# Residual stream held token by token: activations stationary in the out and down projections, LayerNorm per token, normalised tiles turned back

## The reference

```
x = first_block(x)                   # x += mixers(rms_norm(x)) @ w_out;  x += swiglu(rms_norm(x))
for i in range(4):                   # mixers: mLSTM, sliding window, HGRN2, differential attention
    for sub, f in enumerate((mixer[i], swiglu[i])):
        shift, scale, gate = split(silu(c) @ ada_w[i, sub] + ada_b[i, sub])     # 3 vectors of 1024
        h = x * (1 + scale) + shift
        x = layer_norm(ALPHA * x + (1 + gate) * f(h), ln_g[i, sub], ln_b[i, sub])
```

## Time and profile before

| | |
|---|---|
| runs | 3871.58, 3900.40, 3900.23 us, median 3900.23 |
| profiled execution: span | 3867.7 us |
| profiled execution: its own time | not given apart; the run nearest above its span is 3871.58, 3.9 us above it |
| PE busy | 3586.9 us, 93% |
| DVE, ACT, POOL busy | 1707.8 us (44%), 1205.6 us (31%), 1375.9 us (36%) |
| weight transfers | 501 of 512 KB, one of 501 slots each |

### The profile page before, as it was taken

The page is one execution under the profiler, slowest core; times in us unless marked ns, Lnnn a source line. Parts: engine busy times, 40 slices in busy tenths (PEclk is TensorE's granted clock), DMA queues, the critical chain, the costliest instruction groups (busy, mean ns, idle before and its releaser), DMA issues.

```text
span 3867.7 us, 44206 instructions
## 1 busy us (share of the span) xinstructions
PE 3586.9 (93%) x15724; PEld 2727.3 (71%) x15724; DVE 1707.8 (44%) x2681; ACT 1205.6 (31%) x1885; POOL 1375.9 (36%) x671
## 2 busy tenths in 40 slices
PE   7987999999879999899899999778999998989998
PEld 6754578886647888655688868665788875658886
DVE  2244345502155551554555232696654156553211
ACT  3235333222223222323333233332332231533322
POOL 3420034443304444300344434583344532024442
PEclk9868799999889999965899989989999988999998
DMA  4300045532204553200255423201455321012331
GB/s 136 98 22 1 20 144 186 193 113 77 76 0 138 184 186 128 85 17 1 82 195 189 143 79 102 64 1 53 145 184 179 113 79 60 1 44 87 98 98 66
DMA packets 101525, 374.07 MB, mean 97 GB/s; under 512 B 11280, under 2 KB 11408, under 8 KB 101136
## 3 DMA queue, kind: packets, MB, share of 16 engines
q1 hardware_dynamic: 101232, 371.76, 29.0%
q0 software_dynamic: 160, 0.52, 0.0%
HBM read 370.15 MB, written 2.10 MB: 96 GB/s over the span
## 4 chain that ended last, share of the span: by engine, by line
PE 79%; DVE 6%; ACT 2%; POOL 1%; issue 1%; DMA 0%; DVEq 0%; ACTq 0%; POOLq 0%
PE bank L602 18%; PE bank L604 18%; PE bank L603 18%; PE bank L787 4%; PE bank L807 3%; PE bank L690 2%; PE bank L691 2%; PE bank L692 2%; PE bank L795 2%; PE bank L646 1%; PE bank L648 1%; PE bank L647 1%; PE bank L992 1%; POOL hg_t L547 1%; DVE hg_d L1823 1%
## 5 line engine op out<-in xcount | busy, mean ns | idle before, releaser
L519 POOL TENSOR_TENSOR w_lo<-raw,w_hi 128x1024 fp32r<-128x1024 f32 x501 | 1230.8, 2461 | 2421.6 <-ACT w_hi L1086 2421.6
L1086 ACT ACTIVATE w_hi<-raw 128x1024 fp32r<-128x1024 f32 x501 | 527.8, 1058 | 1475.4 <-PE bank L604 1249.0
L602 PE MATMUL bank<-h_hi,w_hi 128*128 128x512 f32 x2392 | 934.6, 391 | 0.0
L604 PE MATMUL bank<-h_hi,w_lo 128*128 128x512 f32 x2392 | 931.8, 390 | 0.0
L603 PE MATMUL bank<-h_lo,w_hi 128*128 128x512 f32 x2392 | 931.5, 389 | 0.0
L602 PEld LDWEIGHTS bank<-h_hi,w_hi 128*128 128x128 f32 x2392 | 449.7, 188 | 94.3 <-issue 1.7
L604 PEld LDWEIGHTS bank<-h_hi,w_lo 128*128 128x128 f32 x2392 | 449.5, 188 | 94.2
L603 PEld LDWEIGHTS bank<-h_lo,w_hi 128*128 128x128 f32 x2392 | 449.7, 188 | 92.5
L1887 DVE SCALAR_TENSOR_TENSOR ada_acc<-ada_raw,cond,ada_acc 128x1024 f32<-128x1024 f32 x168 | 266.1, 1584 | 236.8 <-DMA ada_raw<-ada 235.6
L602 PE MATMUL bank<-hid_hi,w_hi 128*128 128x512 f32 x880 | 343.0, 390 | 0.4 <-DVE hid_lo L1903 0.4
L604 PE MATMUL bank<-hid_hi,w_lo 128*128 128x512 f32 x880 | 342.5, 389 | 0.0
...
## 6 DMA issues: line engine op xcount, KB each, us to landing
raw<-weights SPq DMA_DIRECT2D x501, 512.0 KB, 3.6
ada_raw<-ada SPq DMA_DIRECT2D x192, 512.0 KB, 4.4
layer_const<-layer_const SPq DMA_DIRECT2D x5, 512.0 KB, 4.4
...
```

The source lines that it names most:

```text
L519: nc.gpsimd.tensor_tensor(w_lo[k % RING][:, :, :], raw[k % RING][:, :, :], w_hi[k % RING][:, :, :].bitcast(F32), ALU.subtract).then_inc(sm ...
L602: mm(out, w_hi[r][:, at, :], hi, start=first and at == 0, stop=False)
L604: op = mm(out, w_lo[r][:, at, :], hi, start=False, stop=last and at == len(pairs) - 1)
L1086: fn(w_hi[t % RING][:, :, :], raw[t % RING][:, :, :], ACT.Copy).then_inc(sm.hi_done, 1)
```

## The change

x is held token-major, `[128, 4, 1024]`: token tile t has 128 tokens on the partitions and the 1024 features along the row. In the out and down projections the activations are now the stationary operand (128 features x 128 tokens) and the weights move (128 features x 512 output features). The output is made in two halves e = 0, 1 of 512 features. Within a half the four token tiles accumulate side by side in four banks, input chunk by input chunk (`token_chunk`: 12 products a chunk); in the last half the last four chunks go token by token (`last_half`), so that banks finish one after another. The weights are laid out by halves (`half_slots`); a down projection takes 22 slots instead of 24. The number of products is unchanged, 192 in an out projection and 528 in a down projection.

For each half and token tile DVE multiplies the bank by the gate row (L1587 of the changed kernel), adds ALPHA x (L1590) and takes BN_STATS of the 512 features (L1591). At e = 1 it aggregates the two (BN_AGGR, L1594), ACT takes a 128 x 1 root, DVE inverts it and writes the normalised token tile `xn` (128 x 1024, L1492). PE turns `xn` back to feature-major by 32 transposes of 128 x 128 (matrix products with the identity): 16 before the next projection (L743), 16 between its early products (L754). DVE applies scale and shift on reading the transposed banks (L1518). The gate is needed as a row: DVE writes eight diagonal tiles (L1541), PE spreads them by two float32 products with ones (L805, L806), DVE copies two banks (L1545). LayerNorm's own gain and bias reach x only later, two DVE operations of 128 x 1024 for each token tile, in the first eight `up` tiles of the feed-forward part or the first eight tiles of the next layer's input projection; for this `ln_rows` are loaded as broadcast rows, two transfers of 512 KB for each LayerNorm. After the last down projection gain and bias are applied token by token, each token tile stored by a transfer of its own. x is loaded by four transfers, and the first norm takes its squares on ACT token by token.

Order of PE at the middle of the out projection of the mLSTM layer, changed kernel: the end of the first half (ring buffer w_hi_58), the two gate products, and the beginning of the last half.

Two sums by ones, 32 short products of squares and one spreading product gave way to transposes that wait for one token tile each. The diff, cut to its core:

```diff
-        x = place("x", [P, DT, S], F32)
+        x = place("x", [P, TT, D], F32)
...
+            def first_turns(src):
+                for t in range(TT):
+                    if src is xn:
+                        pe.wait_ge(sm.xn_ready, n["xn"] + t + 1)
+                    for c in range(4):
+                        op = turn(bank[4 + c][:, t * P:(t + 1) * P], src[:, t, c * P:(c + 1) * P], ident)
+                        if t == TT - 1:
+                            op.then_inc(sm.x_turned, 1)
+                n.add(xn=TT if src is xn else 0)
+            def turned_early_tiles(src):
                 for c in range(DT):
+                    if c < 4:
+                        pe.wait_ge(sm.h_ready, n["h"] + c + 1)
+                        for t in range(TT):
+                            op = turn(bank[4 + c][:, t * P:(t + 1) * P], src[:, t, (4 + c) * P:(5 + c) * P], ident)
+                        op.then_inc(sm.x_turned, 1)
...
+            def token_products(k, mt, s, c, t, hi, lo, count):
+                r, d = (k + s) % RING, 2 * s + c
+                w = [ring[r][:, :, :].rearrange("p (c t) m -> p c (t m)", c=2)[:, c, :] for ring in (w_hi, w_lo)]
+                out, tok = bank[(mt + t) % 4][:, :], slice(t * P, (t + 1) * P)
+                if d == 0:
+                    pe.wait_ge(sm.lin_free, mt + t - 3)
+                mm(out, hi[:, d, tok], w[0], start=d == 0, stop=False)
+                mm(out, hi[:, d, tok], w[1], start=False, stop=False)
+                op = mm(out, lo[:, d, tok], w[0], start=False, stop=d == count - 1)
+                if d == count - 1 and t < TT - 1:
+                    op.then_inc(sm.y_done, 1)
+                return op
+            def token_chunk(k, mt, d, hi, lo, count, parts_from=None):
+                s, c = d // 2, d % 2
+                if parts_from is not None:
+                    pe.wait_ge(sm.part_lo, parts_from + d + 1)
+                if c == 0:
+                    pe.wait_ge(sm.lo_done, k + s + 1)
                 for t in range(TT):
...
+                    op = token_products(k, mt, s, c, t, hi, lo, count)
+                if c:
+                    op.then_inc(sm.slot_used, 1)
+            def last_half(hi, lo, count):
+                k, mt, slots = n["slot"], n["mt"], count // 2
+                for d in range(count - 4):
+                    token_chunk(k, mt, d, hi, lo, count)
+                pe.wait_ge(sm.lo_done, k + slots)
+                for t in range(TT):
+                    for s in (slots - 2, slots - 1):
+                        for c in range(2):
+                            op = token_products(k, mt, s, c, t, hi, lo, count)
+                        if t == TT - 1:
+                            op.then_inc(sm.slot_used, 1)
+                n.add(slot=slots, mt=TT)
+            def gate_rows(sub):
+                n.add(gate=1)
+                pe.wait_ge(sm.gate_diag_ready, n["gate"])
+                diag = gate_diag[sub][:, :, :].rearrange("p c f -> p (c f)")
+                mm(bank[4][:, :], ones, diag[:, 0:S], start=True, stop=True)
+                mm(bank[5][:, :], ones, diag[:, S:D], start=True, stop=True).then_inc(sm.gate_spread, 1)
+            def out_projection(part, items):
+                k, mt, c = n["slot"], n["mt"], 0
+                if items:
+                    for t in range(len(items)):
+                        group_sum(items, t)
+                    for t in range(len(items) + 2):
+                        if t < len(items):
+                            group_spread(part, t, (4, 5))
+                        if t >= 2:
+                            for _ in items[t - 2]["src"]:
+                                token_chunk(k, mt, c, h_hi, h_lo, DT, n["part"])
+                                c += 1
+                    n.add(gn=len(items), gq=len(items) // 4)
+                for c in range(c, DT):
+                    token_chunk(k, mt, c, h_hi, h_lo, DT, n["part"])
+                n.add(part=DT, slot=DT // 2, mt=TT)
+                if part != "first":
+                    gate_rows(0)
+                last_half(h_hi, h_lo, DT)
...
+                for d in range(FT):
+                    token_chunk(k, mt, d, hid_hi, hid_lo, FT, n["part"])
+                    if d == 3:
+                        ada_sums(5, 0)
+                    if d == 7 and layer is not None:
+                        gate_rows(1)
+                n.add(part=FT, slot=FT // 2, mt=TT)
+                last_half(hid_hi, hid_lo, FT)
...
+            def token_roots(eps, ready, between=lambda t: None):
+                for t in range(TT):
+                    between(t)
+                    ready(t)
+                    fn(ln_root[:, t:t + 1], ln_mv[:, t, 1:2], ACT.Sqrt, bias=eps).then_inc(sm.x_root, 1)
...
+            def inverse_root(t):
                 n.add(root=1)
-                link(v.memset(rt[1][:, :], 0.0))
-                dve.wait_ge(sm.n_root, n["root"])
-                link(v.reciprocal(rt[0][:, 0:P], rt[0][:, 0:P]))
-                for t in range(TT):
-                    rows = slice(32 * t, 32 * t + 32)
-                    op = v.tensor_copy(rt[1][rows, t * P:(t + 1) * P], rt[0][rows, 0:P])
-                op.then_inc(sm.n_inv, 1)
-                dve.wait_ge(sm.n_spread, n["root"])
-            def rms_input(gain):
-                root()
+                dve.wait_ge(sm.x_root, n["root"])
+                link(v.reciprocal(ln_rstd[:, t:t + 1], ln_root[:, t:t + 1]))
+            def normed_token(t, centred):
+                inverse_root(t)
+                rstd = ln_rstd[:, t:t + 1]
+                if centred:
+                    op = v.tensor_scalar(xn[:, t, :], x[:, t, :], ln_mv[:, t, 0:1], rstd, ALU.subtract, ALU.mult)
+                else:
+                    op = v.tensor_scalar(xn[:, t, :], x[:, t, :], rstd, None, ALU.mult)
+                op.then_inc(sm.xn_ready, 1)
+            def affine_token(sub, t, stage):
+                if stage == 0:
+                    return v.scalar_tensor_tensor(x[:, t, :], x[:, t, :], ln_mv[:, t, 0:1], ln_row[sub][:, 0, :],
+                                                  ALU.subtract, ALU.mult)
+                return v.scalar_tensor_tensor(x[:, t, :], x[:, t, :], ln_rstd[:, t:t + 1], ln_row[sub][:, 1, :],
+                                              ALU.mult, ALU.add)
...
+            def gate_rows(layer, sub):
+                n.add(gate=1)
+                one = mod_col(layer, sub, ONE_GATE, 0, 8)
+                v.tensor_tensor(gate_diag[sub][:, :, :], ident.unsqueeze(1).to_broadcast([P, DT, P]),
+                                one.unsqueeze(2).to_broadcast([P, DT, P]), ALU.mult).then_inc(sm.gate_diag_ready, 1)
+                dve.wait_ge(sm.gate_spread, n["gate"])
+                for e in range(2):
+                    op = v.tensor_copy(gate_row[sub][:, e * S:(e + 1) * S], bank[4 + e][:, :])
+                op.then_inc(sm.gate_row_kept, 1)
+                dve.wait_ge(sm.gate_row_kept, n["gate"])
...
-            def add_residual(slots, layer=None, sub=None, part_sum=None):
-                if layer is not None:
-                    n.add(xs=DT)
-                    dve.wait_ge(sm.x_scaled, n["xs"])
-                for m in range(DT):
-                    b = tile_done(slots)
-                    if layer is None:
-                        v.tensor_tensor(x[:, m, :], b[:, :], x[:, m, :], ALU.add).then_inc(sm.lin_free, 1)
-                    else:
-                        v.scalar_tensor_tensor(x[:, m, :], b[:, :], mod_col(layer, sub, ONE_GATE, m), x[:, m, :],
-                                               ALU.mult, ALU.add).then_inc(sm.lin_free, 1)
-                        dve.wait_ge(sm.lin_free, n["mt"])
-                        if 1 <= m < DT - 1:
-                            op = v.tensor_tensor(part_sum[:, :], part_sum[:, :] if m > 1 else x[:, 0, :], x[:, m, :], ALU.add)
-                            if m < DT - 2:
+            def add_residual(slots, layer=None, sub=None, after=lambda t: None):
+                for e in range(2):
+                    for t in range(TT):
+                        n.add(mt=1)
+                        if t < TT - 1:
+                            n.add(y=1)
+                            dve.wait_ge(sm.y_done, n["y"])
+                        else:
+                            n.add(slot=slots // 2)
+                            dve.wait_ge(sm.slot_used, n["slot"])
+                        b, xs = bank[(n["mt"] - 1) % 4], x[:, t, e * S:(e + 1) * S]
+                        if layer is None:
+                            v.tensor_tensor(xs, b[:, :], xs, ALU.add).then_inc(sm.lin_free, 1)
+                        else:
+                            y = gated[sub][t % 2][:, :]
+                            v.tensor_tensor(y, b[:, :], gate_row[sub][:, e * S:(e + 1) * S],
+                                            ALU.mult).then_inc(sm.lin_free, 1)
+                            dve.wait_ge(sm.lin_free, n["mt"])
```

(13 more changed lines are left out.)

388 lines of the change are left out of this document (185 added, 203 removed).

## The result

The changed kernel takes **3945.7 us** (median of four runs, 3934.7 to 3954.5) against 3895.7 for the kernel before: a ratio of 1.0139, 95% interval 1.0097 to 1.018. It is slower by 1.4%. The forecast was 3927, some 27 us slower, and the range 3866 to 3988; the direction was right and the loss was about twice as large. (The forecast was set on a median before of 3900.2 from three runs; a fourth has since lowered it to 3895.7.)

What follows compares the result with a forecast made beforehand. PE, busy 93%, was taken as the bound: its work and the places where it stands. Out projections' LayerNorms +25.2, down projections' +3.3, the last -2.3, first block +1.2 made +27 us: 3927 against 3900.23; 8-in-10 range 3866 to 3988.

Steps and rivals of the forecast that it cites:

- seven gaps: PE's gap at each of seven LayerNorms: 10.7 us instead of 18.5, -7.8 us each.
- transposes between early tiles, seven: Sixteen transposes between the early products of the next projection: +2.2 us at each LayerNorm.
- four out projections: gate, middle, clock: In each out projection: gate rows +2.1 us, PE's wait for banks between the halves +7.2, slow clock after it +2.6.
- three down projections: gate, middle, clock: In each down projection: gate rows +2.1 us, PE's wait for banks between the halves +3.6, slow clock +1.0.
- last down projection: In the final down projection: gate rows +2.1 us, wait for banks between the halves +3.6, slow clock +1.0.
- first block to layer 0's early tiles: First block: shorter second norm, its transposes +2.2 us, input transposes +2.0, start +0.9; together +1.2.
- gain and bias in up tiles: Two DVE passes of 1.28 us over eight tiles of 5.44 us, hidden beside the next projection's products: no cost.
- Rival A: Gaps shrink to 9.0 us and banks are free in time, so faster: 3856 to 3884 us; chance 0.25.
- D: The LayerNorm gap does not shorten, as DVE's and POOL's contention takes what the chain gives: 3982 us; chance 0.09.
- rival B: BN_STATS on DVE is slow, at the scan's 1.78 us: 3989 us; chance 0.15.
- Rival C: PE's transposes are dear, at 0.368 us each, 5.2 us a norm: 3979 us; chance 0.10.
- The down projection has two slots fewer but not fewer products: nothing: Down projection: having fewer weight slots with the same products was put at no cost.

Runs made afterwards that it cites:

- Experiment 1: Changed kernel with the last hidden tile's product put ahead of DVE's last four modulation passes: 3931.1 us, ratio 1.0102.
- Experiment 5: Changed kernel with banks emptied before scaled sums, last hidden tile ahead of modulation passes, out projection's gate products earlier, down projection's modulation sum and gate rows moved: 3871.7 us.
- Experiment 4: Changed kernel without the late gain and bias passes of the first seven LayerNorms (output differs): 3916.1 us, ratio 1.0068.
- 6: Experiment 5 with feed-forward gain and bias behind every second up tile: 3862.3 us; then also layer 1's input-projection passes moved into its out projection: 3854.0 us.

## Why the prediction was right or wrong

| step | forecast (us) | measured in the two profiles (us) |
|---|---|---|
| seven gaps | -55 | -57 |
| transposes between early tiles, seven | +15 | +3 |
| four out projections: gate, middle, clock | +48 | +46 |
| three down projections: gate, middle, clock | +20 | +44 |
| last down projection | +7 | +7 |
| tail | -9 | -11 |
| first block to layer 0's early tiles | +1 | +8 |
| gain and bias in up tiles | 0 | +7 |
| input parts and mixers of layers 0 to 3 | 0 | +18 |
| sum | +27 | +65 |

**Right.** That the gap shrinks, to 10.0 with 10.7 forecast, and that the middle of the out projection eats it (so rivals A and D fall): the pieces stand in the trace nearly as worked out (gate row spread by E + 1.9, first bank in PE's hands at E + 5.0, then one each 2.05 us). BN_STATS was taken at 0.6 us and is 0.69, so rival B falls. The middle of the last down projection is 1.08 and 1.81 us of waiting, 1.9 of gate products and some 2.5 that go with the clock; the sum is 7.3 with 6.7 forecast, with less wait and more clock. The out projection's is of the same kind: PE waited 4.3 to 5.6 us and not 7.2. By the prediction's own signs a wait under 3 us in a middle was to count against it, and the 2.9 of the down projection is just that. Rival A falls by its own condition, since the banks were not free in time.

**Transposes** were put too high. Four take 0.60 us between early products, but the early stages grew by only 3 us in seven norms and not by 15. They last 19 to 20 us for 16.3 us of products, so most transposes seem to fall where PE would have waited or run slow anyway; no run here separates the two. Rival C falls with it: sixteen in a row took 1.97 us, 0.12 each, in the changed kernel:

```profile
891.31 1.97 PE L743 MATMUL bank<-kept,x 128*128 128x128 f32 x16 [0.79 <-DVE x L1584]
```

The 275 ns of the Trainium skill ("TensorE: Matmul & The Clock Gate", Part 4) are about the duration of one of these records (276 on the mean), not what one adds: they overlap.

**Wrong: the down projection's start.** The prediction counted four banks at the middle and said that they are full when a half ends. It never asked the same question where a half *begins* behind other work. The step "The down projection has two slots fewer but not fewer products: nothing" failed. The down projections of the first block and of layers 0 to 2 exceed the forecast by 7.7 and 23.8 us, 31 together, and 21.9 of it are the four waits for L1983. Experiment 1 shows the cause by removing these waits: 16.6 us went, and the rest stayed beside new waits for the modulation sum. Experiment 5, which moves that sum too, brings every down projection to within 1.8 us of before; since it makes several edits at once it does not price them apart.

**Wrong: gain and bias at nothing.** The step named the cover (beside products of 5.44 us a tile) and took 1.28 us a pass. It is 1.7 to 1.8 on the mean, with 2.7 and more where a pass meets a split, although the prediction used that very contention for the gap; and it did not count what else DVE has in those tiles, the modulation passes in the feed-forward part and the tables in layer 1. Experiment 4 gives 21 us for it. In the up tiles of layers 0 to 2 PE does not wait for the passes themselves. It waits 0.6 us once, for modulation work that stands behind them on DVE, and the rest of the +2.5, +4.1 and +0.9 us goes with the clock after it; the wait is absent before the change and in experiments 4 and 6. In layer 0 it is this one:

```profile
1271.66 1.95 PE L1058 MATMUL bank<-kept,ada_acc 128*128 128x1 f32 x16 [0.63 <-DVE ada_acc L1970]
```

**The first block** was forecast at +1 and took +8. Without the 7.7 of its down projection the rest would have matched only by chance: its start was put at +0.9 and came 3.8 us earlier, its second norm was to lose 2.6 and kept its 9.0, and its out projection, for which there was no term, is 3.6 shorter. No run tells why.

**Luck.** The measured time lies inside the forecast's own range of 3900 to 3950, by 4 us, although two terms put at nothing cost 52 us in the profiles, twice the whole forecast. That is luck in part: the transposes, 12 us too high, and gaps and tail, 5 us better than forecast, covered a part, and the medians differ by 15 us less than the profiles.

The remainder, +3.6 us in the first block's mixers and +2.5 in layer 0's, is of the size by which equal work differs between profiles, and I count it to no step. One sum of the prediction is off: B, C, D and a tenth of the forecast are 0.38 and not 0.36. Against the medians (+50) the shortfall is 23 us; against the profiles (+65) it is 38, where 31 + 21 stand against 12 too much for transposes and some 5 of the tail and the gaps. The two sums are not to be had more exactly, since a median of before moves by some us from one set of runs to the next (3892.7 to 3898.0).
